# Hymba decoder step on one core: who subtracts the low parts of weight groups 9 to 19

## What is computed

```python
xn = rmsnorm(x, ln1_w)
z = xn @ w_in                       # 1024 x 3592: q, k, v of 8 attention heads, q, k, v, gate of 4 mLSTM heads
attn = moba_attention(qa, k_all, v_all, q_start)
h, C, n, m = mlstm_chunkwise(qm, km, vm, i_pre, f_pre, C0, n0, m0)
x = x + concat(attn, h) @ w_out
x = x + square(relu(rmsnorm(x, ln2_w) @ w_up)) @ w_down
```

## Time and profile before

| | |
|---|---|
| median of 3 runs | 751.14 us (748.95 to 752.32) |
| the profiled execution: its time | 749.44 us |
| its span, first to last instruction | 747.7 us, mean TensorE clock 0.976 |
| PE busy | 699.8 us (94%) |
| DVE busy | 467.4 us (63%) |
| ACT busy | 301.6 us (40%) |
| POOL busy | 294.8 us (39%) |
| HBM | 92.92 MB read, 6.64 MB written, 133 GB/s over the span |
| w_lo on POOL (L1418) | 20 times, 47.5 us busy |
| products on POOL (L1862) | 32 times, 82.8 us busy |

### The profile page before, as it was taken

One profiled execution on the slowest core, in us unless ns is written; L12 is line 12 of the kernel. 1 busy time (PEld: TensorE's weight loads), 2 busy tenths in 40 slices (PEclk: granted clock), 3 DMA queues, 4 the chain that ended last, 5 costly groups with the idle time before them and its releaser, 6 DMA issues.

```text
span 747.7 us, 15193 instructions
## 1 busy us (share of the span) xinstructions
PE 699.8 (94%) x5537; PEld 650.9 (87%) x5537; DVE 467.4 (63%) x932; ACT 301.6 (40%) x576; POOL 294.8 (39%) x215
## 2 busy tenths in 40 slices
PE   5999789797999999889878999999999999999997
PEld 5988678686878787689868999999999999999996
DVE  4387978766352438434987868575756757586133
ACT  5342454533445223125653544435234433534322
POOL 5225987831232335154002361706144160704531
PEclk8999999998999999989989999999999999999999
DMA  7716998742556968821112232423313141332202
GB/s 243 212 46 208 269 282 249 202 144 74 168 147 197 279 196 176 259 83 61 57 57 60 104 122 59 134 92 113 114 57 112 59 163 59 113 113 85 86 1 115
DMA packets 88634, 100.42 MB, mean 134 GB/s; under 512 B 5374, under 2 KB 64338, under 8 KB 88570
## 3 DMA queue, kind: packets, MB, share of 16 engines
q1 hardware_dynamic: 74566, 92.91, 40.1%
q10 hardware_dynamic: 14004, 6.67, 3.5%
HBM read 92.92 MB, written 6.64 MB: 133 GB/s over the span
## 4 chain that ended last, share of the span: by engine, by line
PE 78%; DVE 11%; ACT 4%; issue 2%; DMA 2%; POOL 1%; SPq 0%; ACTq 0%; DVEq 0%; POOLq 0%
PE acc L869 6%; PE acc L870 6%; PE acc L871 6%; PE acc L1335 5%; PE acc L1334 5%; PE acc L1336 5%; PE acc L1321 4%; PE acc L1320 4%; PE acc L1322 4%; PE scr L1335 3%; PE scr L1334 3%; PE scr L1320 3%; PE scr L1336 3%; PE scr L1322 3%; PE scr L1321 3%
## 5 line engine op out<-in xcount | busy, mean ns | idle before, releaser
L869 PE MATMUL acc<-act_hi,w_hi 128*128 128x256 f32 (+1 forms) x416 | 123.8, 298 | 1.1 <-DVE zT L2411 1.1
L870 PE MATMUL acc<-act_lo,w_hi 128*128 128x256 f32 (+1 forms) x416 | 119.0, 286 | 0.0
L871 PE MATMUL acc<-act_hi,w_lo 128*128 128x256 f32 (+1 forms) x416 | 118.9, 286 | 0.0
L1919 POOL TENSOR_TENSOR h_lo<-relu,h_hi 128x520 fp32r<-128x520 f32 x32 | 43.9, 1373 | 187.6 <-ACT h_hi L1735 187.2
L1862 POOL TENSOR_TENSOR prod<-kv,Qb 128x1024 f32<-128x1024 f32 x32 | 82.8, 2614 | 42.9 <-DVE S L2088 25.2
L869 PEld LDWEIGHTS acc<-act_hi,w_hi 128*128 128x128 f32 x416 | 80.2, 193 | 8.1 <-issue 4.8
L1418 POOL TENSOR_TENSOR w_lo<-raw,w_hi 128x1024 fp32r<-128x1024 f32 x20 | 47.5, 2378 | 96.7 <-ACT w_hi L1411 96.7
L870 PEld LDWEIGHTS acc<-act_lo,w_hi 128*128 128x128 f32 x416 | 80.3, 193 | 0.0
L871 PEld LDWEIGHTS acc<-act_hi,w_lo 128*128 128x128 f32 x416 | 80.0, 192 | 0.0
L2430 DVE TENSOR_TENSOR xT<-acc,xT 128x260 f32<-128x260 f32 x64 | 26.4, 427 | 55.1 <-PE acc L1336 55.1
L2411 DVE TENSOR_TENSOR zT<-acc,rstd 128x264 f32<-128x264 f32 (+1 forms) x56 | 23.5, 423 | 55.6 <-PE acc L871 49.6
(11 more groups left out here) (408 smaller groups left out, 2296.3 us busy)
## 6 DMA issues: line engine op xcount, KB each, us to landing
kv<-in_cache_k_dram SPq DMA_DIRECT2D x64, 256.0 KB, 3.2
kv<-in_cache_v_dram SPq DMA_DIRECT2D x64, 256.0 KB, 3.3
raw<-in_w_up_dram SPq DMA_DIRECT2D x16, 1024.0 KB, 5.5
raw_d<-in_w_down_dram SPq DMA_DIRECT2D x12, 1024.0 KB, 5.0
raw<-in_w_in_dram SPq DMA_DIRECT2D x14, 512.0 KB, 6.0
raw<-in_w_in_dram SPq DMA_DIRECT2D x7, 1024.0 KB, 6.8
x_tok<-in_x_prompt_dram SPq DMA_DIRECT2D x8, 512.0 KB, 9.1
raw<-in_w_out_dram SPq DMA_DIRECT2D x4, 1024.0 KB, 6.4
```

What stands on the lines that cost most here:

```text
L869: pe.matmul(out, w_hi[:, slot, k, :], hi[k][:, cols], start=(n == 0), stop=False)
L870: pe.matmul(out, w_hi[:, slot, k, :], lo[k][:, cols], start=False, stop=False)
L871: mm = pe.matmul(out, w_lo[:, slot, k, :], hi[k][:, cols], start=False, stop=(n == KT - 1))
L1919: pool.tensor_tensor(h_lo[:, t, :], relu2[:, t % 2, :], h_hi[:, t, :].bitcast(F32), ALU.subtract).then_inc(s_hs_lo, 1)
```

## The change

A function `lo_on_pool(n)` says which engine makes the low part of group n: GpSimd for groups 0 to 3 and 20 to 35 as before, and now also for the odd groups 9, 11, 13, 15, 17 and 19. VectorE keeps 4 to 8 and the even groups 10 to 18. The subtraction stays at the same slot. Since the count of finished groups must rise in order, each engine waits for the other's group n-1 wherever that was the other's. GpSimd's wait at group 20 falls away, because group 19 is its own.

```diff
--- before.py
+++ after.py
@@ -102,6 +102,11 @@
         return s - 1 if s > WSLOTS else None
     n = s // 2 + AHEAD
     return n if s % 2 == 0 and 2 * WSLOTS <= n < G_MLP else None
+
+
+def lo_on_pool(n):
+
+    return n < WSLOTS or n >= POOL_LO or n % 2 == 1 and n > 8
 
 
 def ml(part, h):
@@ -1902,9 +1907,9 @@
 
             for s in range(N_HALVES):
                 n = split_at(s)
-                if n is not None and n >= POOL_LO:
-                    if n == POOL_LO:
-                        pool.wait_ge(s_w_lo_ok, POOL_LO)
+                if n is not None and lo_on_pool(n):
+                    if not lo_on_pool(n - 1):
+                        pool.wait_ge(s_w_lo_ok, n)
                     weight_lo(pool, n, n % WSLOTS, n // 2 % 2)
                 for name in TASKS[s]:
                     task(*name)
@@ -2474,9 +2479,9 @@
 
             for s in range(N_HALVES):
                 n = split_at(s)
-                if n is not None and n < POOL_LO:
-                    if n == WSLOTS:
-                        dve.wait_ge(s_w_lo_ok, WSLOTS)
+                if n is not None and not lo_on_pool(n):
+                    if lo_on_pool(n - 1):
+                        dve.wait_ge(s_w_lo_ok, n)
                     weight_lo(dve, n, n % WSLOTS, n // 2 % 2)
                 if s == slot_of(0, 1):
                     for name in TASKS[s]:
```

## The result

The changed kernel took 755.11 us in the median of five runs (753.02 to 756.1), the kernel before, on the same chip, 750.38 (747.84 to 752.32, five runs). The ratio is 1.0062, 95% interval 1.0035 to 1.0089: slower by 4.7 us, between 2.6 and 6.7. The profiled execution took 753.02 us; its span is 751.3 us, 3.6 more than that of before. In the changed file the lines behind the new function stand five lower: L1418 is L1423, L1862 is L1867, L1180 is L1185, L1205 is L1210, L1132 is L1137.

A forecast was written before the change was run, and what follows sets the result against it. TensorE, busy 94%, was taken as the bound, with VectorE's lateness ending 12.5 us of its waits; -0.4 + 1.2 + 1.4 = +2.2, taken as +1.9 on the median 751.14, gave 753.0 us, range 747.5 to 758.0.

The forecast's parts named there:

- within 0.5%: Whole kernel: a time not told apart from the kernel before, 0.5% being 3.8 us; chance 0.63.
- L1185, score step of 84.40: At 70 to 104 us: score step starts 1.6 us late, behind group 10 and a score drain on VectorE.
- L1198, step of 102.91: At 102.91 us: TensorE waits for VectorE's late copy of transposed probabilities and leaves the stage 1.5 us late.
- L1091, second half, of 147.24: Near 147 us: group 17 leaves VectorE, the 2.41 us wait goes, TensorE is 3.0 us ahead.
- end of the last product: GpSimd makes group 17 ahead of its last two products, which end at 154.8 us instead of 154.3.
- L1210 starts: Near 157 us: the score drain behind group 18 frees its bank at 156.9 instead of 157.26, gain 0.4 us.
- slow clock in L1210's stage: After a pause of about 4 us near 157 us, slower matmuls cost 1.4 us, between nothing and 2.5.
- gate chain and group 19: At 157 to 177 us: subtraction leaves VectorE (-1.1), a gate operation is held by GpSimd's (+2.3); net +1.2 us.
- sum, at L1137 and behind it: -0.4 + 1.2 + 1.4 = +2.2 us, taken as +1.9 since TensorE may find slack.
- After 180 us ... I let the shift reach the end: Behind 180 us: moved groups and products are over, MLP half untouched, so the shift reaches the end unchanged.
- GpSimd as the bound (2): Among the products: GpSimd's added work makes the last reduction 6.7 us late; +5.9, up to +8, 757 to 759; chance 0.26.
- VectorE's relief lasting (3): TensorE keeps the 3.0 us won at 147 us, group 19 misses the gate chain: -5.5, 745.6; chance 0.12.

The follow-up runs named there:

- e9: The changed kernel itself, unchanged, profiled in one more single execution: 752.11 us.
- e7: Against the changed kernel, only group 17 of the six goes to GpSimd: 754.04 us, ratio to the kernel before 1.0044.
- e3: The changed kernel, with GpSimd making group 19 behind slot 32's tasks instead of ahead of them: 750.47 us, ratio to the kernel before 1.0012.
- e8: The kernel before, unchanged, in a second profiled single execution: 747.96 us.
- e5: Against the changed kernel, VectorE keeps 4 to 16, GpSimd makes 17 and up, 19 after slot 32's tasks: 748.73 us, ratio to before 0.9976.
- e6: Against the changed kernel, VectorE keeps 4 to 17, GpSimd makes 18 and up, 19 after slot 32's tasks: 748.73 us, ratio to before 0.9957.
- e11: Repeat of the code with 18 and up on GpSimd and 19 made after slot 32's tasks: 747.74 us, ratio to the kernel before 0.9973.
- e10: Against the changed kernel, GpSimd makes group 18 and 20 to 31; 19 and 4 to 17 stay on VectorE: 749.35 us, ratio to before 0.9986.
- e2: Against the changed kernel, only group 19 of the six goes to GpSimd: 751.71 us, ratio to the kernel before 1.0024.
- e4: Against the changed kernel, only groups 9 and 11 of the six go to GpSimd: 751.98 us, ratio to the kernel before 1.0016.

## Why the prediction was right, and where it wasn't

The forecast was +1.9 us against the median, within its range of 747.5 to 758.0; measured were +4.7 (2.6 to 6.7). The sign came out as forecast, the size as 4.7 where 1.9 was forecast. The likeliest class was "within 0.5%"; the result is 0.62%, with an interval of 0.35 to 0.89%.

Its steps, in us since the first reduction, from the two profiled executions:

| step of the prediction | predicted shift | measured |
|---|---|---|
| L1185, score step of 84.40 | +1.6 | +1.05 at its start; the half behind it starts +2.3, ends +2.9 |
| L1198, step of 102.91 | +1.5 | +0.5 |
| L1091, second half, of 147.24 | -3.0 | -2.7 |
| end of the last product | +0.5 | +0.7 |
| L1210 starts | -0.4 | -0.1 |
| slow clock in L1210's stage | +1.4 | +1.6 (3.90 us to the next half, 2.30 before) |
| gate chain and group 19 | +1.2 | +0.9 |
| sum, at L1137 and behind it | +2.2 | +2.4 |

**The sum held, and for its reasons.** Group 17's gain of 3 us at 147 was lost ten microseconds later, at the place named. The port was as exclusive as the earlier trace rows suggested. The term that hung most on a choice between far bounds was the gate chain's +2.3, taken because the start times coincided: it measured 2.31 less 0.22, 2.1 us. The slow clock behind L1210 was a choice too, 1.4 between nothing and 2.5; it measured 1.6, 1.45 in e9 and 2.2 in e7, so that it fitted this well is in part luck. The Trainium skill's rule that the second engine is fully blocked (page "SBUF — State Buffer", section "Who interferes with whom") is what this row shows, and e3, where the two no longer meet, takes it away.

**The early stage was sized wrongly.** "The 1.5 us at L1193 is set by VectorE's queue, and what TensorE loses before it comes off its wait there" left out the clock at the score step: after a pause of 4.88 us the stretch from 80 to 90 us shows 0.66, and TensorE was 2.9 us late at the end of the next half. The wait forecast at L1193 isn't there: the changed kernel's profile has none at the step of 102.91, e9's has 0.25 us. TensorE's lateness came to 0.5 by 102 us for a reason that the prediction doesn't have: in the kernel before, TensorE stood twice near 98 us for ScalarE's copies, and in the changed kernel, being late, it didn't. That the early stage left the sum standing is luck, not the prediction's reasoning. TensorE's timeline of before:

```profile
97.43 0.55 PE L1193 MATMUL scr<-ident,pr 128*128 128x128 f32 x3 [0.46 <-ACT k_stage L1479]
99.57 0.60 PE L908 MATMUL scr<-ident,zT 128*8 128x128 f32 x4 [1.60 <-ACT v_tok L1479]
```

The prediction read only the waits that VectorE ended. It also priced each moved group at the median, 6 x 1.64 = 9.8 us; the six that moved took 13.1 in the trace (2.25, 1.75, 3.00, 2.61, 2.23 and 1.22), and it left out that those which stay grow longer.

**The step that failed** is "After 180 us ... I let the shift reach the end". It added nothing there, where 2.6 us came on top (II +2.3, IV +0.3); with e9 against e8 it is 2.3. That is about the difference between forecast and result, 2.8 us, as far as two executions of each kernel can say. Of the 2.3 us in II, 0.5 lie ahead of the wait on a transfer near 305 us, 0.3 in it, and 1.5 behind it, where the clock was at 0.66. The prediction had treated that stage as following TensorE's own order; executions of one code differ there by 1.7 us. Whether the changed kernel meets the long wait more often stays open.

**The rivals.** GpSimd as the bound (2) is out: its last product came 0.7 us later, not 6.7. Its extra 10 us of work went into pauses, as argued from the earlier trace rows. VectorE's relief lasting (3) didn't come, since group 18 didn't get in ahead of the last product. What it describes is reached by e5 and e6 in another way, with group 18 off VectorE and group 19 clear of the gate chain: 1.8 to 3.2 us faster than before by the ratios of e5, e6 and e11 (2.0 to 2.8 by the medians), not the 5.5 that the rival was priced at.

## What to carry to other kernels

When two engines share a port, moving an operation from one to the other pays where it lands beside nothing with two inputs on the other engine, or beside something that nobody waits for (group 19 in e3): one such subtraction costs 0.4% in front of the last products (e7), and another costs nothing that can be measured behind them (e10). Ask of each moved operation what stands behind it in its new queue and who waits for that, and move the one that meets nothing; here two well-placed ones (e6, e11) beat six taken in turns. A wait that vanishes counts only once the next thing that TensorE needs has been found and shown to be early.

## What the runs showed that was not expected

- The cost of a pause goes on after it. After 4.88 us of wait four matmuls took 2.08 us instead of 1.13; with 4.05 us in e7 the two stretches from 155 to 165 us show 0.64 and 0.67. After the 1.92 us pause of e5 it was 1.00.
- It isn't the same each time: in the kernel before, a pause of 1.60 us near 98 us was followed by a clock of 1.00 in one execution, one of 1.65 us by 0.50 from 100 to 102 us in the other (e8). That is worth 1.4 us from slot 19 on. The wait at L1193 takes up none of it (1.78 us in both); it shrinks to 0.56 by slot 31 because e8 keeps its clock behind the 2.41 us wait near 147 us, where the other execution lost it. Of the five executions with both pauses (before, e8, e2, e10, e11) two lost the clock at the first, three at the second, none at both.
- The MLP half, whose code is the same in all kernels, took 355.0 to 355.3 us in ten of the thirteen executions, but 356.5 in e4 and e7 and 357.5 in e5. A span alone, from one execution, can't rank versions that lie 1 or 2 us apart.
- A small loss can cancel another: being 2.9 us late, TensorE skipped a wait of 2.1 us on ScalarE and the slow clock that may follow it.
